# One 512-column matmul for both parts of the tokens in the expert tables, with the sum made at eviction

## The reference

```python
def peer(h, wq, keys, u_tab, v_tab):          # blocks of 128 tokens
    q = (hblk @ wq).reshape(128, 8, 2, 128)   # 8 heads, 2 halves
    s = einsum('nhpd,hpkd->nhpk', q, keys)    # 128 keys per half
    top_s, top_i = top_k(s, 16)
    cand_s = top_s[:, :, 0, :, None] + top_s[:, :, 1, None, :]
    best_s, best_pos = top_k(cand_s, 16)      # 16 of 256 pairs per head
    idx = take(top_i[0] * 128 + top_i[1], best_pos)
    gate = softmax(best_s)
    act = gelu(einsum('nd,nhkd->nhk', hblk, u_tab[idx]))
    return einsum('nhk,nhkd->nd', gate * act, v_tab[idx])
```

## Time and profile before

| | us |
|---|---|
| median of 3 runs | 2424.6 (2424.23 to 2431.13) |
| profiled execution, device time | 2426.12 |
| its span, first to last instruction | 2424.8 |
| TensorE busy | 2322.7 |
| VectorE busy | 1810.6 |
| ScalarE busy | 1121.8 |
| GpSimd busy | 171.6 |

### The profile page before, as it was taken

How to read it: one execution, slowest core, us unless ns; L and a number is a source line. 1 busy time by engine, 2 the same in 40 slices (tenths; PEclk the granted TensorE clock), 3 DMA queues, 4 the chain that set the end, 5 groups by cost and what they waited for, 6 DMA issues and landing times.

```text
span 2424.8 us, 39043 instructions
## 1 busy us (share of the span) xinstructions
PE 2322.7 (96%) x15710; PEld 2050.9 (85%) x15710; DVE 1810.6 (75%) x3279; ACT 1121.8 (46%) x1615; POOL 171.6 (7%) x79
## 2 busy tenths in 40 slices
PE   8799999998899999999999999999999999999997
PEld 6689987775799999998777777799999998777786
DVE  8658987557658777778888878748877777887656
ACT  5446554346444444444444444344444444444443
POOL 0000000000014330000000000003440000000000
PEclk9879999998999999999999999999999999999999
DMA  8326675322455555455557886455555545556663
GB/s 317 110 71 223 194 285 192 96 70 96 140 174 183 166 183 166 166 167 169 170 173 286 308 332 223 145 183 174 166 187 168 168 166 168 172 170 225 216 214 121
DMA packets 123202, 442.58 MB, mean 183 GB/s; under 512 B 13696, under 2 KB 16768, under 8 KB 122256
## 3 DMA queue, kind: packets, MB, share of 16 engines
q1 hardware_dynamic: 117288, 425.04, 51.5%
q10 hardware_dynamic: 5736, 15.06, 1.8%
HBM read 436.88 MB, written 3.16 MB: 181 GB/s over the span
## 4 chain that ended last, share of the span: by engine, by line
PE 82%; DVE 11%; ACT 4%; issue 2%; DMA 1%; ACTq 0%; SPq 0%; DVEq 0%
PE ps L400 26%; PE ps L401 25%; PE ps L402 25%; PE ps L2462 3%; DVE spl L2248 2%; ACT spl L961 1%; DVE acc L1537 1%; DVE cv L1801 1%; PE ps L2407 1%; ACT cv L1211 1%; PE ps L428 1%; DVE hT L1517 1%; PE ps L626 0%; DVE sm L2026 0%; DVE ex L1951 0%
## 5 line engine op out<-in xcount | busy, mean ns | idle before, releaser
L2248 DVE TENSOR_TENSOR spl<-ring,spl 128x1024 fp32r<-128x1024 f32 (+1 forms) x639 | 779.3, 1221 | 450.8 <-ACT spl L961 448.7
L961 ACT ACTIVATE spl<-ring 128x1024 fp32r<-128x1024 f32 x703 | 736.9, 1051 | 366.5 <-PE ps L402 344.0
L400 PE MATMUL ps<-hT,spl 128*128 128x256 f32 x2656 | 767.3, 289 | 18.7 <-DVE spl L2248 17.1
L401 PE MATMUL ps<-hT,spl 128*128 128x256 f32 x2656 | 757.7, 285 | 0.0
L402 PE MATMUL ps<-hT,spl 128*128 128x256 f32 x2656 | 757.3, 285 | 0.0
L400 PEld LDWEIGHTS ps<-hT,spl 128*128 128x128 f32 x2656 | 515.6, 194 | 24.7 <-DVE spl L2248 21.0
L401 PEld LDWEIGHTS ps<-hT,spl 128*128 128x128 f32 x2656 | 516.7, 195 | 0.0
L402 PEld LDWEIGHTS ps<-hT,spl 128*128 128x128 f32 x2656 | 516.0, 194 | 0.0
L400 PE MATMUL ps<-spl,Ws 128*128 128x512 f32 x1024 | 412.6, 403 | 4.9 <-DVE Ws L2256 4.7
L401 PE MATMUL ps<-spl,Ws 128*128 128x512 f32 x1024 | 405.7, 396 | 0.0
L402 PE MATMUL ps<-spl,Ws 128*128 128x512 f32 x1024 | 405.3, 396 | 0.0
(11 more groups left out here) (373 smaller groups left out, 2347.2 us busy)
## 6 DMA issues: line engine op xcount, KB each, us to landing
ring<-in_peer_u SPq DMA_DIRECT2D x256, 512.0 KB, 3.5
ring<-in_peer_v SPq DMA_DIRECT2D x256, 512.0 KB, 3.5
vring<-in_ada_w SPq DMA_DIRECT2D x56, 512.0 KB, 6.3
ring<-in_w_up SPq DMA_DIRECT2D x44, 512.0 KB, 4.3
aring<-in_ada_w SPq DMA_DIRECT2D x40, 512.0 KB, 6.1
ring<-in_ab_in SPq DMA_DIRECT2D x32, 512.0 KB, 3.4
ring<-in_peer_wq SPq DMA_DIRECT2D x32, 512.0 KB, 4.0
ring<-in_w_down SPq DMA_DIRECT2D x22, 512.0 KB, 6.3
```

The costliest lines, as they stand in the source:

```text
L400: q.matmul(o, l[0], r[0], start=start, stop=False)
L401: q.matmul(o, l[0], r[1], start=False, stop=False)
L961: q.activation(P.spl[:, m % SPLITS, 0, 0:w], P.ring[:, m % SLOTS, 0:w], ACT.Copy).then_inc(*P.hi.mark(m))
L2248: q.tensor_tensor(P.spl[:, n % SPLITS, 1, 0:w], P.ring[:, n % SLOTS, 0:w], P.spl[:, n % SPLITS, 0, 0:w].bitcast(F32), ALU.subtract).then_i ...
```

## The change

- `mm3_both` takes the place of `mm3` for the query tiles and the first table. High x (high and low tokens) is one matmul of 512 columns into a whole bank: high x high in columns 0 to 255, high x low in 256 to 511. Low x high, 256 columns, is added to columns 0 to 255. In the last step of a tile the short one goes first.
- So a tile needs a bank of its own, a pair two. The queries use banks 0 to 3, the first table the bank pairs (1,2), (4,5), (6,7) in turn. The two halves are added at eviction: ScalarE copies the second halves of both banks to `S` or `qT` (`act_u2`), VectorE adds the first halves (`dve_u`, `dve_query`), and for the table ScalarE applies the GELU in place in `S`. The adds are issued behind a low part (`dve_sums`).
- Order on ScalarE in the first table: cast, copy of the last pair, cast, GELU of the pair before that.
- The scores are computed in two groups of 32 matmuls, after query tiles 11 and 15.
- In the search, the indices and the comparison matrix are in half precision; the 128 positions are written twice side by side. One more low part is issued after 8 of the first 16 maxima.
- In the second table VectorE reads the folded modulation columns three tiles later than before (`dve_ada_cols`). The gates of the first 8 tokens of the second half are multiplied before the low part of the third `v` tile, not behind it.

```diff
+SC_AFTER = {11: ((0, 0), (0, 4), (1, 0), (1, 4)), 15: ((0, 8), (1, 8), (0, 12), (1, 12))}
+U_BANK = (1, 4, 6)
-        self.ps = [nc.alloc_psum_tensor(f"ps{i}", [128, 512], F32) for i in range(8)]
+        self.psum = nc.alloc_psum_tensor("psum", [128, 8, 512], F32)
+        self.ps = [self.psum[:, i, :] for i in range(8)]
+def mm3_both(q, b, l, r, start, stop):
+    if not stop:
+        q.matmul(b[:, :].rearrange("p (z t) -> p z t", z=2), l[0], r, start=start, stop=False)
+        return q.matmul(b[:, 0:256], l[1], r[:, 0], start=False, stop=False)
+    q.matmul(b[:, 0:256], l[1], r[:, 0], start=False, stop=False)
+    return q.matmul(b[:, :].rearrange("p (z t) -> p z t", z=2), l[0], r, start=False, stop=True)
@@ act_peer, queries and scores
         if f % 2:
+            b = 2 * (f // 2 % 2)
             q.wait_ge(*pe.at(("q", f // 2)))
-            q.activation(P.qT[:, f - 1:f + 1, :].rearrange("p a t -> p (a t)"), P.ps[f // 2 % 4][:, :],
-                         ACT.Copy).then_inc(*act.mark(("q", f // 2)))
+            q.activation(P.qT[:, f - 1:f + 1, :], P.psum[:, b:b + 2, 256:512], ACT.Copy).then_inc(
+                *act.mark(("q2", f // 2)))
+        for tb, g0 in SC_AFTER.get(f, ()):
+            ...
@@ act_peer, first table
     for p in range(32):
-        act_u(q, P, l, p)
+        act_hi(q, P, T + 16 + 2 * p + 2)
+        if p:
+            act_u2(q, P, l, p - 1)
+        act_hi(q, P, T + 16 + 2 * p + 3)
+        if p >= 2:
+            act_u(q, P, l, p - 2)
...
+def act_u2(q, P, l, p):
+    b = U_BANK[p % 3]
+    q.wait_ge(*pe.at(("u", p)))
+    q.activation(P.S[:, 2 * p:2 * p + 2, :], P.psum[:, b:b + 2, 256:512], ACT.Copy).then_inc(*act.mark(("u2", p)))
+def act_u(q, P, l, p):
+    q.wait_ge(*dve.at(("us", p)))
+    s = P.S[:, 2 * p:2 * p + 2, :].rearrange("p j t -> p (j t)")
+    q.activation(s, s, ACT.Gelu_apprx_tanh).then_inc(*act.mark(("gelu", p)))
@@ dve_route_top
         q.max(P.vals[:, g, 0:8], sc[:, g, :]).then_inc(*dve.mark(("v", tb, g)))
+        if g == 7:
+            dve_lo(q, P)
...
-        q.tensor_tensor(e3, bc(P.iot[:, 0:16].unsqueeze(1), [128, 128, 16]),
-                        bc(P.bq[:, z, :].unsqueeze(2), [128, 128, 16]), ALU.is_equal).then_inc(*dve.mark())
+        q.tensor_tensor(e2, bc(P.iot16[:, 0:16].rearrange("p (a e) -> p a e", e=2).unsqueeze(1), [128, 128, 8, 2]),
+                        bc(P.bq[:, z, :, :].unsqueeze(2), [128, 128, 8, 2]), ALU.is_equal).then_inc(*dve.mark())
@@ dve_lo, after a low part
+            dve_sums(q, P, n)
+def dve_sums(q, P, n):
+    for l, T in enumerate(T_PEER):
+        if T + 4 <= n < T + 16 and (n - T) % 2 == 0:
+            dve_query(q, P, l, (n - T - 4) // 2)
+        if T + 16 <= n < T + 146:
+            while P.sum_next[l] <= (n - T - 16) // 2 - 2:
+                dve_u(q, P, l, P.sum_next[l])
+def dve_u(q, P, l, p):
+    b = U_BANK[p % 3]
+    x = P.S[:, 2 * p:2 * p + 2, :]
+    q.wait_ge(*act.at(("u2", p)))
+    q.tensor_tensor(x, P.psum[:, b:b + 2, 0:256], x, ALU.add).then_inc(*dve.mark(("us", p)))
@@ dve_peer
+    dve_u(q, P, l, 63)
+    dve_gates(q, P, 1, 0, pe, act, dve)
...
         dve_ws(q, P, j, act, dve)
+        dve_ada_cols(q, P, ("v", l, j - 3))
         dve_ada(q, P, ("v", l, j))
@@ pe_peer, queries
-            t = mm3(q, P.ps[f // 2 % 4][:, f % 2 * 256:f % 2 * 256 + 256],
-                    cut(sl, lambda v: v[:, k * 128:(k + 1) * 128]), cut(both(P.hT), lambda v: v[:, k, :]),
-                    k == 0, k == 7)
+            t = mm3_both(q, P.ps[f % 4], cut(sl, lambda v: v[:, k * 128:(k + 1) * 128]), P.hT[:, :, k, :],
+                         k == 0, k == 7)
@@ pe_u
-    q.wait_ge(*act.at(("gelu", p - 2) if p >= 2 else ("q", 5 + p)))
+    if p >= 3:
+        q.wait_ge(*dve.at(("us", p - 3)))
+    elif p:
+        q.wait_ge(*act.at(("sc", p - 1, 12)))
+    else:
+        q.wait_ge(*dve.at(("q", 7)))
```

More of the change, by code:

```diff
@@ L1540, in dve_ada, with dve_ada_cols @@
                     *P.ada_dve.mark(("acc", z, i), ("acc", 1, i), ("step", i)))
-        elif ADA_TASK[i][1] not in (2, 5):
+    if slot[0] != "v":
+        dve_ada_cols(q, P, slot)
+def dve_ada_cols(q, P, slot):
+    for kind, i in ADA_PLAN.get(slot, []):
+        if kind == "fold" and ADA_TASK[i][1] not in (2, 5):
             l, qn = ADA_TASK[i]
@@ L2393, in pe_peer @@
                 q.wait_ge(*dve.at(("lo", k)))
[L2394 to L2396 removed]
+            t = mm3_both(q, P.ps[f % 4], cut(sl, lambda v: v[:, k * 128:(k + 1) * 128]), P.hT[:, :, k, :],
+                         k == 0, k == 7)
         t.then_inc(*pe.mark(("used", n), *([("q", f // 2)] if f % 2 else [])))
[L2398 to L2410 removed]
+        for tb, g0 in SC_AFTER.get(f, ()):
+            q.wait_ge(*P.line(f"keys{g0 // 8}_loaded").at((l, g0 // 8)))
+            q.wait_ge(*dve.at(("q", g0 // 2 + 1)))
+            q.wait_ge(*(act.at(("sc", tb, g0 - 8)) if g0 >= 8 else b4dve.at(("y", tb, g0 // 4))))
+            for g in range(4):
+                t = q.matmul(P.ps[4 + 2 * tb + g0 // 4 % 2][:, g * 128:(g + 1) * 128],
+                             P.qT[:, g0 + g, tb * 128:(tb + 1) * 128],
+                             P.keys[:, (g0 + g) * 128:(g0 + g + 1) * 128], start=True, stop=True)
+            t.then_inc(*pe.mark(("sc", tb, g0)))
     for p in range(32):
```

85 lines of the change are left out of this document (44 added, 41 removed).

## The result

| | before | changed |
|---|---|---|
| median, us | 2424.61 (2424.23 to 2431.13, 4 runs) | 2394.23 (2393.91 to 2395.13, 4 runs) |
| ratio, 95% interval | | 0.9869 [0.9852, 0.9886] |
| span of the profiled execution, us | 2424.8 | 2392.6 |

A forecast was written before the change was run, and what follows sets the result against it. TensorE's matmul pace plus its few stops was taken to bound the kernel. Terms 30.3 + 8.1 + 7.0 + 1.4 - 0.4 = 46.4 us, off the profiled 2426.1, gave 2379 as median; range for 8 in 10: 2360 to 2402.

The forecast's parts named there:

- the first rival: Query and first-table tiles: long matmul paced like the weighted-activation one, 15.2 us from the matmuls, time 2393; chance 0.22.
- merged matmuls: Query and first-table tiles: one instruction fewer per step saves 13.3 ns over 2272 steps, 30.3 us.
- low part after 8 maxima: Start of the second token half's search: shorter TensorE stop saves 3.0 us, less half clock 5.1; sum 8.1.
- columns read later: Second table: VectorE no longer waits for the fold, saving 3.6 us of stops and 3.4 of clock; 7.0.
- scores split: Around the last four query tiles: the 0.69 us wait before the scores goes, 1.4 us over two layers.
- first one-hot build later: Behind the scores: each table's first one-hot build comes one sum closer to its deadline, 0.2 us worse, twice.
- sums, search: First table: adds at eviction are hidden, and neither adds nor half-precision search are on the path; 0 us.
- The lower bound, 15.2: Query and first-table matmuls: 6.7 ns saved a step if the long one takes 233.3 ns, 15.2 us in all.
- The rival of two separate stretches: Long matmul reads high and low tokens as two stretches, taking 240 ns; matmuls gain nothing, time 2408; chance 0.06.
- the one with a pace of 333 ns: Matmul steps: a long matmul hides the weight load, 60.6 us saved, 2348, half the extra likelier, 2363; chance 0.11.
- the forecast's lower bound of 3.0: Second search's beginning: 1.5 us of TensorE stop saved twice, without the 5.1 us counted for the clock.
- The slower rival: Second half of a table: VectorE becomes the bound once an add exceeds 1.3 us; 2456 at 2.5 us; chance 0.05.

The follow-up runs named there:

- run 1: The changed kernel with each 512-column matmul issued as two of 256 columns with the same weights: 2412.7 us, ratio 0.9951.
- run 3: The changed kernel without the low part after 8 of 16 maxima: 2400.41 us, ratio 0.9908.
- run 4: The changed kernel with the folded modulation columns read right behind the fold's tile, as before the change: 2402.2 us, ratio 0.9912.
- run 5: The changed kernel with all 64 score matmuls in one block behind the sixteenth query tile: 2394.71 us, ratio 0.9872.
- run 6: The changed kernel with the search's table of matches in 32 bits again: 2414.48 us, ratio 0.9945.
- run 2: The changed kernel with high and low parts of the tokens side by side in memory: 2392.81 us, ratio 0.9878.
- run 9: The changed kernel with the first one-hot build of each table ahead of the low part of tile 65: 2391.76 us, ratio 0.986.
- run 10: The changed kernel with the first one-hot build ahead of tile 65's low part, and one low part issued while VectorE waits for the routing transposes: 2384.52 us, 0.983.
- run 7: The changed kernel with a second VectorE instruction of 512 elements behind each of the 128 sums of the first tables: 2468.3 us, ratio 1.0175.
- L S, S L: The changed kernel with long (L) and short (S) matmuls in this order over pairs of steps, not strictly in turn: 2389.62 us, ratio 0.985.

## Why the prediction was right, and where not

The sign was right, and the time lies inside the range, but 15 us above the value. The forecast's own number for the first rival, 2393, is closer, though not by that rival's way. Step by step:

| step | forecast, us | measured, us |
|---|---|---|
| merged matmuls | 30.3 | 18.5 (run 1) |
| low part after 8 maxima | 8.1 | 5.2 in the trace, 6.2 in the medians (run 3) |
| columns read later | 7.0 | 7.9 in the trace, 8.0 in the medians (run 4) |
| scores split | 1.4 | 1.4 of waiting is gone, but only 0.1 a layer by the split (run 5) |
| first one-hot build later | -0.4 | -3.2 (2 x 0.83, and 1.5 of clock; by subtraction from the stretches) |
| sums, search | 0 | near 0, by two large effects (run 6) |

The measured column adds up to about 30 us, which is what the change takes off.

*Matmuls: the term that was mis-sized.* The step "if the long one has the fixed part of the token-weight row: 226.7 + 120.0" added two paces, each read in a run of equal matmuls. In alternation they do not add: 352.5 ns a step and not 346.7. The first half saves 7.5 ns a step and the second 9.2, instead of 13.3; over 2272 steps that is 18.8 us, and run 1 has 18.5. The lower bound, 15.2, held. The first rival (the pace of the weighted-activation row) has the right number for the step, 353.3, but not its parts (233.3 + 120.0): the long ones take 231 ns in a row and 235 in alternation. The rival of two separate stretches is refuted by the pace (360 by it) and by run 1, and run 2 shows that where the stretches lie doesn't matter; the one with a pace of 333 ns is refuted by all of them.

*The Trainium skill's 2.5 ns.* By the Trainium skill, TensorE: Matmul & The Clock Gate, section "Wait — 56ns, not 53.3ns?", a warm matmul carries about 2.5 ns beside its columns; the estimate from it was 5.7 us for this step. Run 1 measures 18.5, so the figure does not hold for these matmuls, and the measurement decides.

*Stops.* The wait of 1.6 us came out at 1.66 and lost its half-clock stretch. The size is below the forecast's 8.1 since that took the kernel before as the measure, with 6.8 us of half clock behind the first layer's stop. With the stop put back (run 3) the first layer shows 3.4. In the runs here the length of these stretches is not fixed by the length of the stop; the forecast's lower bound of 3.0 allowed for that.

*The first one-hot build.* I wrote "one sum closer to its deadline: 0.2 us worse". The queue was read wrongly: three low parts stand in arrears in front of the build, so two sums come with them, and nothing hides them there. 0.83 us a layer, and behind the longer stop (2.1 us) the clock was down in one layer, which is chance (last section). This is the new wait that took back part of the gain, and runs 9 and 10 show it by taking it away.

*Sums and search: right by two effects that cancelled.* "Neither is on the path: the search ends before TensorE asks for it. I put nothing down." The outcome of that step was near zero, its reason was false, and that it came out was luck. The search does end early, but the low parts that TensorE needs after each pair are issued between the search's instructions on the same engine. VectorE was at 72.36 of 87 us in that half before; it is at 76.57 of 84 now. Without half precision the same change is 20 us slower (run 6), and as a whole it would have given 12 (2426.1 beside it, 2414.5).

*The slower rival.* Its threshold, 1.3 us an add, and its place, the second half, were both wrong. With 1.33 us per sum (0.72 and 0.61 with the extra instruction, from start to start in run 7) the second half lost 3 us in a layer, 0.1 us a round: VectorE waits about 1 us in each round of the changed kernel, and the extra 0.7 us fitted into that. The first half, which the rival didn't look at, made that kernel 42 us slower than before. Its support was misread too: the rows of 4.38 us for a product and 1.48 for 128 elements are not prices of the instructions alone; they hold a wait for GpSimd. In the changed kernel's trace, VectorE and GpSimd:

```profile
771.01 1.23 DVE L2225 TENSOR_TENSOR eq<-iot,bq 128x2048 f16<-128x2048 f16 x1
772.27 3.31 DVE L2228 TENSOR_TENSOR eq<-eq,idx 128x2048 f16<-128x2048 f16 x1
```
```profile
771.59 2.91 POOL L2606 TENSOR_TENSOR spl<-ring,spl 128x1024 fp32r<-128x1024 f32 x1 [3.23 <-ACT spl L979]
```

The compare ends at 772.24, GpSimd at 774.50, the product 1.08 us after that. All eight products of the changed kernel take 3.31 us, against 1.23 for those in run 7 that met no GpSimd work: 2.1 us each, 17 us of VectorE in all.

## What to carry to other kernels

- Merging two matmuls that share their weights pays by the instruction's fixed part, but read that part in the mix in which the matmul will run: two paces from runs of equal sizes gave 346.7 ns, the alternation 352.5, and the order L S, S L 349.5.
- An engine's total says little where its queue mixes something that another engine waits for with something that nobody waits for. Ask at each deadline what is in arrears in front of it; one low part put into an engine's idle wait (run 10) took off 7.2 us more than moving the build alone (run 9).
- A mean far above what an instruction of its size takes elsewhere (4.38 us against 2.29) can be a wait in disguise; look at what the neighbouring engine does in that moment before using it as a price.
